# Expert units of up to 288 rows with the final norm inside, in place of blocks of 128 rows and a closing stage

## The reference

```python
def expert_block(args):
    xb_i, e = args
    h = jax.nn.silu(xb_i @ w_gate[e]) * (xb_i @ w_up[e])
    return h @ w_down[e]
...
y = h + hier_moe(hn, ...)          # sum over the row's two experts, each times its weight
...
y_prompt = rmsnorm(hp, g_final)
y_sample = rmsnorm(hs, g_final)
```

## Time and profile before

| | us |
|---|---|
| median of 3 runs | 2057.92 |
| lowest and highest run | 2057.64, 2058.57 |
| span of the profiled execution | 2054.1 |
| PE busy | 1895.9 (92%) |
| DVE busy | 1034.9 (50%) |
| ACT busy | 832.3 (41%) |
| POOL busy | 283.8 (14%) |

### The profile page before, as it was taken

How to read it: one execution, slowest core, us unless ns; L and a number is a source line. 1 busy time by engine, 2 the same in 40 slices (tenths; PEclk the granted TensorE clock), 3 DMA queues, 4 the chain that set the end, 5 groups by cost and what they waited for, 6 DMA issues and landing times. The chain is left out here.

```text
span 2054.1 us, 28746 instructions
## 1 busy us (share of the span) xinstructions
PE 1895.9 (92%) x9892; PEld 1600.8 (78%) x9893; DVE 1034.9 (50%) x2051; ACT 832.3 (41%) x1564; POOL 283.8 (14%) x388
## 2 busy tenths in 40 slices
PE   6999999999999999999997764999999999999980
PEld 5788888888878888888885543888888888888870
DVE  4644455544454544555444654454456454546434
ACT  4333333333343333333323553444446454446423
POOL 2000000010000010000100202222222222222223
PEclk9999999999999999999997886999999999999995
DMA  6332333323342223522334575585566576656428
GB/s 213 123 100 85 139 140 132 103 92 135 123 145 96 90 83 131 173 77 95 103 123 166 169 250 168 149 268 162 155 224 218 169 264 191 184 174 215 142 53 340
DMA packets 173306, 316.24 MB, mean 154 GB/s; under 512 B 9757, under 2 KB 92701, under 8 KB 173226
## 3 DMA queue, kind: packets, MB, share of 16 engines
q1 hardware_dynamic: 155754, 255.07, 36.0%
q0 software_dynamic: 15120, 51.59, 10.1%
q10 hardware_dynamic: 2352, 8.52, 1.0%
HBM read 266.09 MB, written 49.07 MB: 153 GB/s over the span
## 5 line engine op out<-in xcount | busy, mean ns | idle before, releaser
L751 DVE TENSOR_TENSOR wl<-raw,wh 128x512 fp32r<-128x512 f32 x440 | 274.3, 685 | 207.2 <-ACT wh L573 205.3
L1597 PE MATMUL bank<-gu_hi,ex_hi 128*128 128x256 f32 (+1 forms) x960 | 310.5, 323 | 4.5 <-DVE gu_lo L1507 4.5
L60 PE MATMUL bank<-xT_hi,wh 128*128 128x512 f32 x768 | 301.0, 392 | 10.6 <-ACT ext L711 7.0
L1599 PE MATMUL bank<-gu_hi,ex_lo 128*128 128x256 f32 (+1 forms) x960 | 307.1, 320 | 0.0
L1598 PE MATMUL bank<-gu_lo,ex_hi 128*128 128x256 f32 (+1 forms) x960 | 306.9, 320 | 0.0
L62 PE MATMUL bank<-xT_hi,wl 128*128 128x512 f32 x768 | 299.4, 390 | 0.0
L61 PE MATMUL bank<-xT_lo,wh 128*128 128x512 f32 x768 | 299.3, 390 | 0.0
L573 ACT ACTIVATE wh<-raw 128x512 fp32r<-128x512 f32 x440 | 240.2, 619 | 99.5 <-PE bank L1140 49.9
L1597 PEld LDWEIGHTS bank<-gu_hi,ex_hi 128*128 128x128 f32 x960 | 183.2, 191 | 23.9 <-DVE gu_lo L1507 6.5
L1599 PEld LDWEIGHTS bank<-gu_hi,ex_lo 128*128 128x128 f32 x960 | 183.2, 191 | 13.3
L1598 PEld LDWEIGHTS bank<-gu_lo,ex_hi 128*128 128x128 f32 x960 | 183.5, 191 | 12.5
(11 more groups left out here) (239 smaller groups left out, 3258.0 us busy)
## 6 DMA issues: line engine op xcount, KB each, us to landing
raw<-in_w_in SPq DMA_DIRECT2D x70, 1024.0 KB
raw_gate_up<-in_w_gate SPq DMA_DIRECT2D x16, 2048.0 KB, 8.4
raw_gate_up<-in_w_up SPq DMA_DIRECT2D x16, 2048.0 KB, 13.4
raw_d<-in_w_down SPq DMA_DIRECT2D x16, 2048.0 KB, 13.0
raw<-in_w_out SPq DMA_DIRECT2D x20, 1024.0 KB
raw<-in_w_up_pool SPq DMA_DIRECT2D x20, 512.0 KB
raw<-in_w_up_gmlp SPq DMA_DIRECT2D x20, 512.0 KB
h<-in_x_prompt SPq DMA_DIRECT2D x16, 512.0 KB, 5.2
```

What stands on the lines that cost most here:

```text
L60: nc.tensor.matmul(out, lh, rh, start=(i == 0), stop=False)
L751: lo = lambda out, x, hi: tt(out, x, hi.bitcast(F32), ALU.subtract)
L1597: nc.tensor.matmul(out, a[0][:, ka, :], w[0][:, kw, cols], start=(n == 0), stop=False)
L1599: return nc.tensor.matmul(out, a[1][:, ka, :], w[0][:, kw, cols], start=False, stop=(n == total - 1))
```

## The change

The blocks of 128 rows become units of up to 288 rows: two tiles of 128 and a tail of 32. An expert gets one unit for each 288 rows begun. Gate and up products now have the weights stationary (eight slices of 128 columns in a ring of four) and the 288 rows streaming, so that the hidden values come out transposed and aren't transposed again. The down product has the hidden rows stationary, in the order first tile, second tile, tail; the first tile and the tail use one pair of PSUM banks, the second tile the other. The tail's high and low part lie side by side as 64 stationary columns, and their two halves of the result are added afterwards.

The final norm moves into the unit. The rows of `h` are gathered, the weighted result is added in SBUF, squares, mean, power and the product with `g_final` follow at once, and the rows are scattered: the sum back to `h_rows` (for the row's later expert) and the normed row to the outputs. Each slot now has five fields: row, weight, and three destinations, where a destination beyond the bound is left out; so `h_rows` is written only by a row's first expert and the outputs only by its second. `phase_four` goes, as do the spare zero rows of `h` and `hn`. `place` computes the extra fields with a few more small operations, and the slot table grows from 34816 entries of two fields to 36864 of five. The unit table has entries for 32 units and is computed at the start of `phase_three`.

```diff
+TAIL = 32
+CAP = 2 * P + TAIL
+UPE = -(-(SEQ + SAMPLE) // CAP)
+SLOTS_PER_EXPERT = UPE * CAP
+NSLOT = NE * SLOTS_PER_EXPERT
+UNITS = 32
...
+    slot_dram = nc.dram_tensor("slot_table", [NSLOT, FIELDS], I32).ap()
...
-        phase_four(nc, shared)
...
+    bankB, bankY = psum[0:4], psum[4:8]
+
+    TILES = [(0, P), (P, P), (2 * P, TAIL)]
+    ORDER = (0, 1, 2)
+    Y_OF = ((0, 1), (2, 3), (0, 1))
+    X_PARTS = [(0, 0), (0, 1), (1, 0), (1, 1), (2, None)]
+    NX = len(X_PARTS)
+    SLICES = 2 * KH
+    RING = 4
...
+                with sp.Fori(0, total) as u:
...
+                    for t in range(3):
+                        sp.wait_ge(x_in[t], 16 * u + 16)
+                    sp.wait_ge(cur_ok, 2 * u + 2)
+                    load_slots(base)
+                    sp.wait_ge(w_lo, SLICES * u + SLICES - 1)
                     sp.dma_start(raw_gu[:, 0:KD, :], view(v["w_gate"])).then_inc(gate_in, 16)
+                    sp.wait_ge(w_lo, SLICES * u + SLICES)
                     sp.dma_start(raw_gu[:, KD:2 * KD, :], view(v["w_up"])).then_inc(up_in, 16)
+                    sp.wait_ge(d_lo, KH * u + KH)
                     sp.dma_start(raw_d[:, :, :], view(v["w_down"])).then_inc(down_in, 16)
...
+                with pool.Fori(0, total) as u:
+                    nc.gpsimd.tensor_copy(cur[:, 0:2, :], nxt[:, 0:2, :]).then_inc(cur_ok, 1)
+                    nc.gpsimd.tensor_copy(cur[0:TAIL, 2, :], nxt[0:TAIL, 2, :]).then_inc(cur_ok, 1)
+                    wait_apart(pool, cur_ok, 2 * u + 2, passed_pool)
+                    gather(hrow, h_dram, cur, h_in)
+                    wait_apart(pool, x_tr, NX * u + NX, passed_pool)
+                    wait_apart(pool, slots_in, 32 * u + 64, passed_pool)
+                    gather(x, hn_dram, nxt, x_in)
+                    for i, t in enumerate(ORDER):
+                        n = TILES[t][1]
+                        wait_apart(pool, ms_ok, 3 * u + i + 1, passed_pool)
+                        nc.gpsimd.tensor_tensor(rs[0:n, t:t + 1], ms[0:n, t:t + 1], half_neg[0:n, :], ALU.pow)\
+                            .then_inc(rs_ok, 1)
+                        scatter(h_dram, hrow, t, 2, SEQ + SAMPLE - 1, h_back)
+                        wait_apart(pool, out_ok, 3 * u + i + 1, passed_pool)
+                        scatter(v["y_prompt"][0], out, t, 3, SEQ - 1, y_out)
+                        scatter(v["y_sample"][0], out, t, 4, SAMPLE - 1, y_out)
+                    wait_apart(pool, h_back, 48 * u + 48, passed_pool)
+                    wait_apart(pool, y_out, 96 * u + 96, passed_pool)
...
+                with act.Fori(0, total) as u:
+                    for m in range(KH):
+                        act.wait_ge(gu_done, SLICES * u + 2 * m + 1)
+                        nc.scalar.activation(sg[m % 2][:, :], bankB[2 * (m % 2)][:, 0:CAP], ACT.Sigmoid).then_inc(sg_ok, 1)
+                        if m < 2:
+                            split(u, RING + 2 * m)
+                        if m == 0:
+                            act.wait_ge(down_in, 16 * u + 16)
+                        nc.scalar.activation(dn[0][:, m, :], raw_d[:, m, :], ACT.Copy).then_inc(d_hi, 1)
+                        act.wait_ge(hid_ok, KH * u + m + 1)
+                        nc.scalar.activation(H[:, m, 0:CAP], hid[m % 2][:, :], ACT.Copy).then_inc(H_hi, 1)
+                        if m < 2:
+                            split(u, RING + 2 * m + 1)
+                    rows_high(u + 1, 0)
+                    rows_high(u + 1, 1)
+                    split(u + 1, 0)
+                    rows_high(u + 1, 2)
+                    rows_high(u + 1, 3)
+                    square(u, 0)
+                    split(u + 1, 1)
+                    rows_high(u + 1, 4)
+                    split(u + 1, 2)
+                    square(u, 1)
+                    split(u + 1, 3)
+                    act.wait_ge(y_done, 3 * u + 3)
+                    for c, b in enumerate(Y_OF[2]):
+                        nc.scalar.activation(low[:, c * HALF:(c + 1) * HALF], bankY[b][TAIL:2 * TAIL, :], ACT.Copy)\
+                            .then_inc(low_ok, 1)
+                    square(u, 2)
...
+                def weigh(u, i):
+                    t = ORDER[i]
+                    n = TILES[t][1]
+                    dve.wait_ge(h_in[t], 16 * u + 16)
+                    dve.wait_ge(cur_ok, 2 * u + 2)
+                    if t < 2:
+                        dve.wait_ge(y_done, 3 * u + i + 1)
+                    else:
+                        for c, b in enumerate(Y_OF[t]):
+                            dve.wait_ge(low_ok, 2 * u + c + 1)
+                            tt(low[:, c * HALF:(c + 1) * HALF], bankY[b][0:TAIL, :], low[:, c * HALF:(c + 1) * HALF],
+                               ALU.add)
+                        dve.drain()
+                    for c, b in enumerate(Y_OF[t]):
+                        cols = slice(c * HALF, (c + 1) * HALF)
+                        last = stt(hrow[0:n, t, cols], bankY[b][0:n, :] if t < 2 else low[:, cols],
+                                   cur[0:n, t, 1:2].bitcast(F32), hrow[0:n, t, cols], ALU.mult, ALU.add)
+                    last.then_inc(y_read, 1)
...
+                with dve.Fori(0, total) as u:
+                    for m in range(KH):
+                        pair = 2 * (m % 2)
+                        dve.wait_ge(sg_ok, KH * u + m + 1)
+                        tt(sg[m % 2][:, :], bankB[pair][:, 0:CAP], sg[m % 2][:, :], ALU.mult).then_inc(g_read, 1)
+                        if m < 2:
+                            split(u, RING + 2 * m)
+                        dve.wait_ge(d_hi, KH * u + m + 1)
+                        minus(dn[1][:, m, :], raw_d[:, m, :], dn[0][:, m, :]).then_inc(d_lo, 1)
+                        dve.drain()
+                        dve.wait_ge(gu_done, SLICES * u + 2 * m + 2)
+                        tt(hid[m % 2][:, :], bankB[pair + 1][:, 0:CAP], sg[m % 2][:, :], ALU.mult).then_inc(hid_ok, 1)
+                        dve.wait_ge(H_hi, KH * u + m + 1)
+                        minus(H[:, m, CAP + TAIL:], hid[m % 2][:, 0:2 * P], H[:, m, 0:2 * P])
+                        minus(H[:, m, CAP:CAP + TAIL], hid[m % 2][:, 2 * P:], H[:, m, 2 * P:CAP]).then_inc(H_lo, 1)
+                        if m < 2:
+                            split(u, RING + 2 * m + 1)
+                    rows_low(u + 1, 0)
+                    rows_low(u + 1, 1)
+                    weigh(u, 0)
+                    split(u + 1, 0)
+                    rows_low(u + 1, 2)
+                    rows_low(u + 1, 3)
+                    mean(u, 0)
+                    split(u + 1, 1)
+                    final(u, 0)
+                    rows_low(u + 1, 4)
+                    weigh(u, 1)
+                    split(u + 1, 2)
+                    mean(u, 1)
+                    split(u + 1, 3)
+                    final(u, 1)
+                    weigh(u, 2)
+                    mean(u, 2)
+                    final(u, 2)
...
+                def down(u, t, ks):
+                    hi, lo = t * P, CAP + TAIL + t * P
+                    for k in ks:
+                        pe.wait_ge(H_lo, KH * u + k + 1)
+                        pe.wait_ge(d_lo, KH * u + k + 1)
+                        for c, b in enumerate(Y_OF[t]):
+                            half = slice(c * HALF, (c + 1) * HALF)
+                            last = three(bankY[b][:, :], (H[:, k, hi:hi + P], H[:, k, lo:lo + P]),
+                                         (dn[0][:, k, half], dn[1][:, k, half]), k == 0, k == KH - 1)
+                    return last
...
+                            both = H[:, k, 2 * P:CAP + TAIL]
+                            nc.tensor.matmul(bankY[b][0:2 * TAIL, :], both, dn[0][:, k, half], start=(k == 0), stop=False)
+                            last = nc.tensor.matmul(bankY[b][0:2 * TAIL, :], both, dn[1][:, k, half], start=False,
+                                                    stop=(k == KH - 1))
...
+                with pe.Fori(0, total) as u:
+                    pe.wait_ge(x_lo, NX * u + NX)
+                    for s in range(SLICES):
+                        pe.wait_ge(w_lo, SLICES * u + s + 1)
+                        if s >= RING:
+                            pe.wait_ge(hid_ok if s % 2 else g_read, KH * u + s // 2 - 1)
+                        for k in range(KD):
+                            last = three(bankB[s % RING][:, 0:CAP],
+                                         (gu[0][:, s % RING, k, :], gu[1][:, s % RING, k, :]),
+                                         (xT[0][:, k, :], xT[1][:, k, :]), k == 0, k == KD - 1)
+                        last.then_inc(gu_done, 1)
+                    pe.wait_ge(y_read, 3 * u + 1)
+                    down(u, 0, range(3))
+                    pe.wait_ge(g_read, KH * u + 3)
+                    rows_of_x(u + 1, 0)
+                    pe.wait_ge(hid_ok, KH * u + 3)
+                    rows_of_x(u + 1, 1)
+                    down(u, 0, range(3, KH)).then_inc(y_done, 1)
```

(45 more changed lines are left out.)

548 lines of the change are left out of this document (180 added, 368 removed).

## The result

The changed kernel takes 2039.87 us (median of 4 runs, 2037.62 to 2040.52) against 2058.24 for the kernel before beside it: ratio 0.9909, 95% interval 0.9893 to 0.9925. It is faster, by 18 us where 79 were forecast, and outside the range. Its profiled execution has a span of 2038.3 us.

A forecast was written before the change was run, and what follows sets the result against it. TensorE's matrix instructions were taken to bound the expert stage. Span 2054.1 - 40.0 + 4.8 - 41.4 - 2.5 + 0.8 = 1975.8, plus 3.8 for the runs' median: 1979 us, range 1964 to 2024.

The forecast's parts named there:

- Units and paces: Expert stage on TensorE: 16 units of 43.1 us, 288-column products 0.1334 us each; 40.0 us less than before.
- allowance of 0.35: Per unit on TensorE: 0.35 us added to 42.75 for seven semaphore waits and the loop's edge.
- The end: Behind the last tail product: 15.5 us instead of 56.9, a gain of 41.4 us (bounds 36 and 45).
- The start: Before the first product: 2.5 us gained (from -5 to +5); phase one's sample group placing 0.8 us longer (0 to 1.5).
- The clock loss of 2.8 stays: Start of the expert stage: TensorE still loses 2.8 us to the lower clock there.
- What hides the rest: Inside a unit: other engines and loads stay covered by TensorE; VectorE's slice splits have margins of 0.9 and 1.3 us.
- The rows of x: GpSimd's gather for the next unit: issued at 19.5 us, landed 24 to 27.8, wanted at 29.7.
- The up load: SP's weight load: issued 21 us into the unit, landing 13.4, there at 34.5; its split may slip to 38.8.
- both have come by t = 16: SP's queue: the waits for x and cur, ahead of the gate load, are over 16 us into the unit.
- Rival A: GpSimd's serial round brings the next unit's x late: 8.3 us a unit, 133 in all, 2112 us; chance beyond 79 us 0.09.
- Rival B: VectorE's chain from tail to slices 5 and 7 runs longer: 32 us, 2011; chance with the first rival in part 0.22.
- The rule on the shared port: GpSimd and two-input VectorE instructions exclude each other: 18 us more GpSimd a unit by the rule, 6 by the trace's maximum.

The follow-up runs named there:

- halves_xprev: The changed kernel with each gate and up weight loaded in two column halves and the x rows gathered a round earlier: 1978.59 us, ratio 0.9608.
- before_again: The kernel before the change, profiled once more unchanged: the transposes of the sample group's normed rows begin at 1229.62 us, against 1226.68 in its first trace.
- gate_ahead: The changed kernel with the gate load ahead of the slot load in SP's queue: 2128.05 us, ratio 1.0329 to the kernel before.
- h_early: The changed kernel with the scatter of the h sum issued ahead of the power in GpSimd's queue: 2057.59 us, ratio 0.9990 to the kernel before.
- x a round earlier: The changed kernel with the next unit's x rows gathered a GpSimd round earlier, h scatter and weight loads unchanged: 2006.67 us, ratio 0.9757 to the kernel before.
- the halves: The changed kernel with gate and up weights loaded in two column halves, the first issued early in the unit: 2025.35 us, ratio 0.9839 to the kernel before.

## Why the prediction was wrong

Its own span was to be 1975.8 and was 2038.3: 62.5 more. Of these 5.1 lie ahead of the first product (1268.28, where the forecast's terms give 1263.1), 55.0 in the units (752.2 from first to last tail product, where 697.2 follow from the forecast's terms), 2.4 behind.

- **Units and paces: right.** Sixteen units; a 288-column step 0.133; the sum of products 42.75 is the period of halves_xprev, so the allowance of 0.35 was not needed. That it fits to the hundredth is luck: in one unit of halves_xprev, start to start, the 64 down products take 14.96 for 14.56, the 16 large transposes 1.58 for 2.08, the 8 small ones 0.61 for 0.5.
- **The end: right in kind.** 17.9 us from the last tail product, forecast 15.5, bounds 36 and 45 of gain; the gain is 39.0.
- **The start: half right.** From phase one's marker to the first product it is 35.6 instead of 38.2, the 2.5 forecast. But phase one ends 6.0 us later, for which 0.8 stood (0 to 1.5). Some 3 of them may be variation, as before_again shows: that trace too is behind the first one, by 1.3 us at 105 and 3.1 at 1160, and the changed kernel is level with it, within 0.8 us, until then. The 3.1 us that it loses against before_again come after 1160, in the last 70 us of phase one; which of the added operations or the wider slot table makes them wasn't tried. "The clock loss of 2.8 stays" was wrong: the first unit ran at 1.00 and took 42.87 us.
- **"What hides the rest": the step that failed.** The margins on VectorE were right: in halves_xprev the splits of slices 4, 5 and 7 are done at t = 10.7, 15.2 and 21.1, forecast 10.7, 15.1 and 21.1. The two transfers were mis-sized.
 - *The rows of x*, landed 24 by forecast (wanted 29.7), came at 33.7 in the unit shown. The round's copy came at 19.1 instead of 15.0: 1.5 from a later final(2), the rest from the tail's scatter of 4.5 us for the 1.3 assumed, less a quicker landing. Three h gathers and the way to x took 6.1 instead of 4.5; landing took 8.6 instead of 4.4. 4.1 + 1.6 + 4.2 = 9.9.
 - *The up load*, landed 34.5 by forecast, allowed to slip to 38.8, came at 41.9: issued at 22.6 for 21, and 19.3 us instead of 13.4. The earlier trace rows gave a price measured where a block's transfers were spread out. I multiplied the bytes to a mean of 240 GB/s and compared that with the 387 at the end; but the mean of 205 that was measured is 375 for 21 us behind ten us with next to nothing (0 and 13 GB/s).
 - *SP's queue*: "both have come by t = 16" was wrong, cur came at 19.3; the gate stood behind it 2.6 us.
- **The clock**: the sum had none for waits inside the stage, and one of 2.8 at its start that did not come. TensorE was idle for 43.9 us and busy for 708.4, against 684.0 in sixteen units of 42.75. Of these 24.4 more, 19.3 are the clock: 38.6 us of work at 0.50, half of it lost. The other 5.1 lie at the edges of the waits, where the records' lengths don't overlap. 43.9 and 24.4, less 10.4 of allowances and the 2.8, are the 55.
- **Rival A** named the right mechanism, GpSimd's serial round before x, and priced it at 8.3 us a unit; it was 1.9 to 3.1 of waiting and, in the mean, 1.3 of clock. It put the point of decision at 5 us a unit; gate_ahead waits 8 and is slower than before by 67 us. **Rival B's** place saw waits of 0.6 to 0.9 us in five units, but as the end of the ring of the up load, not from hand-overs: with the load lightened or halved they are gone.
- **The rule on the shared port** (the Trainium skill, SBUF — State Buffer, section "SBUF: two separate sides") had been weighed as at most 6 us a unit. The row of 4.52 us lies where VectorE works from 1649.16 to 1653.70 with one gap of 0.17, and ends 0.14 us after that; in the last unit, with nothing on VectorE behind the final multiply, the same scatter takes 1.89. h_early tried it: the scatter that left this place took 0.89, and the one that came into it 2.51. The rule bites hard on this one transfer of fifteen and a little on others (the unit's last output scatter takes 1.78, and 0.86 in the last unit); most are not held (output scatters 0.99 median). The section names VectorE's two-port modes for held descriptor writing; here the work was arithmetic on two tensors, in two of its five operations with one of them in PSUM. Which of its properties holds the scatter, the runs don't show.

The two theories were each right in part and wrong in that one alone would do. From the change, x a round earlier gives 33 us, the halves 14.5, both 61: 13.6 more than their sum, since each wait that goes leaves the other. (The ratios to the kernel before beside each give 31, 14 and 62.) Only with both is TensorE never idle. That halves_xprev comes out at the forecast's 1979 is partly chance: its units are 13 us shorter than reckoned, its start 7 later, its end (24.0 us, with three spare gathers of x) 8 longer.

## What to carry to other kernels

When a change makes TensorE's work shorter, write every load as a ring: from when its buffer comes free, through a landing time at the rate of the burst it will be in, to the last product that waits; compare the sum with the new period. A landing time read in the old kernel is good only for its old neighbours, and two margins that draw on one burst are one margin.

In a DMA queue a small load that an engine waits for belongs ahead of the large ones: here that held the gate load up by 2.6 us, and the other order cost 88 us in all (gate_ahead against the change).

## What the hardware showed that was not expected

- A 5 KB load took 1.8 us to land ahead of a 2 MB load and 9.0 behind it in one queue.
- An indirect scatter of 32 rows took 4.52 us of GpSimd in fifteen units and 1.89 in the sixteenth, and the DMA share was 0.00 meanwhile. Issued where VectorE had next to nothing to do it took 0.89, and the scatter that took its place beside VectorE's work took 2.51.
- A wait of 3.0 us of TensorE cost twice its length (unit 49.6 us), one of 2.1 little more than itself (45.4): behind the first the granted clock was 0.50 for 5.9 us and eight transposes took 1.94 us instead of 1.04. Ten of fifteen waits of 1.9 to 3.1 us brought the clock down for a while and five didn't, and the shorter ones were not always the harmless ones.
